# A two-layer hybrid block on one core: four-tile routing in fewer VectorE steps, the shared expert's products in quarters, and one direction's pairs of heads made ready one after the other

## The reference

```python
for l in range(DEPTH):
    last = l == DEPTH - 1
    hx = modulate(rmsnorm(x, g_mix[l]), ...)            # hc likewise from ctx
    y_x, y_c = hybrid_mixer(hx, hc, ..., not last)      # attention, mLSTM, RWKV7; merged, @ w_out
    x = x + mod_x[2] * y_x
    hx = modulate(rmsnorm(x, g_ffn[l]), ...)
    f = moe_ffn(hx and, but for the last layer, hc)
    x = x + mod_x[5] * f
return rmsnorm(x, g_final)

# the third branch, in each direction d = 0, 1:
w = -jax.nn.softplus(-(w0[d] + jnp.tanh(wl_d) @ w2[d])) - 0.5
decay, a = jnp.exp(-jnp.exp(w)), jax.nn.sigmoid(a0[d] + al_d @ a2[d])
kd = k * (1 + (a - 1) * k_a)
# and behind both: (norm(y) + bonus) * (sigmoid(gl) @ g2), the output gate

def moe_ffn(xf, ...):                                   # 64 experts, 8 groups
    scores = jax.nn.sigmoid(xf @ w_router)
    # the 4 best groups, then the 8 best experts in them
    _, eidx = lax.top_k(masked, TOP_K)
    wts = scores[eidx] / sum * ROUTED_SCALE
    return routed_experts(xf, eidx, wts, ...) + swiglu(xf, w_s_gate, w_s_up, w_s_down)
```

## Time and profile before

| | |
|---|---|
| median of 3 runs | 2645.62 us (2644.52 to 2645.91) |
| the profiled execution's own time | 2642.83 us |
| its span, first to last instruction | 2640.6 us |
| mean granted clock of TensorE | 0.953 |
| moved by DMA | 599.72 MB, mean 227 GB/s |
| chain that ended last | PE 82%, DMA 7%, DVE 5%, issue 3%, ACT 2% |

### The profile page before, as it was taken

The page is one execution under the profiler, slowest core; times in us unless marked ns, Lnnn a source line. Parts: engine busy times, 40 slices in busy tenths (PEclk is TensorE's granted clock), DMA queues, the critical chain, the costliest instruction groups (busy, mean ns, idle before and its releaser), DMA issues.

```text
span 2640.6 us, 41238 instructions
## 1 busy us (share of the span) xinstructions
PE 2402.9 (91%) x17286; PEld 1365.7 (52%) x17286; DVE 785.4 (30%) x1929; ACT 570.4 (22%) x1132; POOL 146.3 (6%) x154
## 2 busy tenths in 40 slices
PE   7999988999998898999998799988999799967997
PEld 3466477644445443333333556767788644433444
DVE  1364455311114431111111525555411521111112
ACT  3455223300002011111111144433210111100111
POOL 0000000000000111111111000000000011100100
PEclk9999999999997799999999899999999699988999
DMA  7101142411102699999999631122331599999993
GB/s 321 71 10 41 37 157 103 188 64 64 64 0 110 243 422 420 413 406 424 403 408 393 260 146 67 70 70 94 143 147 64 204 393 423 419 408 417 413 423 163
DMA packets 67640, 599.72 MB, mean 227 GB/s; under 512 B 13182, under 2 KB 13310, under 8 KB 25600
## 3 DMA queue, kind: packets, MB, share of 16 engines
q1 hardware_dynamic: 50032, 555.09, 51.9%
q0 software_dynamic: 17424, 41.99, 4.2%
HBM read 588.63 MB, written 26.75 MB: 233 GB/s over the span
## 4 chain that ended last, share of the span: by engine, by line
PE 82%; DMA 7%; DVE 5%; issue 3%; ACT 2%; another core or an unknown queue 0%; SPq 0%; ACTq 0%; DVEq 0%
PE bank L1870 10%; PE bank L1345 9%; PE bank L2296 7%; PE bank L292 6%; PE bank L1885 5%; PE bank L2310 3%; PE bank L1360 3%; PE bank L1350 3%; PE bank L2316 3%; PE bank L384 3%; DMA ring<-in_wexp 2%; DMA arena<-in_wexp 2%; PE bank L1034 2%; PE bank L1049 2%; PE bank L309 1%
## 5 line engine op out<-in xcount | busy, mean ns | idle before, releaser
L1870 PE MATMUL bank<-ring,arena 128*32 128x512 f32 (+2 forms) x1248 | 297.5, 610 | 16.5 <-issue 15.2
L1345 PE MATMUL bank<-normed,ring 128*128 128x512 f32 (+1 forms) x768 | 255.5, 486 | 0.0
L2296 PE MATMUL bank<-ring,arena 128*32 128x512 f32 (+2 forms) x832 | 193.4, 621 | 18.1 <-issue 16.6
L1345 PEld LDWEIGHTS bank<-normed,ring 128*128 128x128 f32 x768 | 145.9, 190 | 101.8 <-issue 91.8
L1870 PEld LDWEIGHTS bank<-ring,arena 128*32 128x32 f32 (+2 forms) x1248 | 94.7, 131 | 154.0 <-issue 152.0
L292 PE MATMUL bank<-normed,ring 128*128 128x512 f32 (+1 forms) x416 | 160.5, 544 | 0.0
L1870 PE MATMUL bank<-branches,arena 128*32 128x512 f32 (+2 forms) x400 | 134.3, 594 | 6.3 <-issue 6.3
L1885 PE MATMUL bank<-arena 128*32 128x512 f32 (+2 forms) x384 | 112.8, 596 | 7.0 <-DMA arena<-in_wexp 3.3
L292 PEld LDWEIGHTS bank<-normed,ring 128*128 128x128 f32 x416 | 78.4, 190 | 77.8 <-issue 75.3
L2060 DVE TENSOR_TENSOR arena<-bank,arena 128x256 f32<-128x256 f32 x43 | 18.3, 425 | 324.0 <-ACT arena L1979 324.0
L2296 PE MATMUL bank<-normed,arena 128*32 128x512 f32 (+1 forms) x256 | 92.9, 644 | 21.0 <-issue 18.1
(11 more groups left out here) (484 smaller groups left out, 3828.5 us busy)
## 6 DMA issues: line engine op xcount, KB each, us to landing
ring<-in_wexp SPq DMA_DIRECT2D x87, 2048.0 KB, 14.5
ring<-in_wst SPq DMA_DIRECT2D x54, 2048.0 KB, 8.4
arena<-in_wexp SPq DMA_DIRECT2D x70, 1024.0 KB, 20.4
branches<-in_wexp SPq DMA_DIRECT2D x31, 2048.0 KB, 13.8
ring<-in_wexp SPq DMA_DIRECT2D x60, 1024.0 KB, 12.1
normed<-in_wexp SPq DMA_DIRECT2D x12, 2048.0 KB
arena<-expert_rows SPq DMA_DIRECT2D x6, 2048.0 KB, 11.0
branches<-expert_rows SPq DMA_DIRECT2D x2, 2048.0 KB, 14.4
```

The lines of the kernel that those rows point to most:

```text
L1345: last = nc.tensor.matmul(ps[2 * (n % 4)][:, c0:], wg[:, k, i * P:(i + 1) * P], H[:, k, c0:], start=(k == 0), stop=(k == KD - 1))
L1870: last = nc.tensor.matmul(ps[2 + s][r0:r1, :], XT_[:, s, k * P + r0:k * P + r1], wt[:, k, :], start=(k == 0), stop=(k == KD - 1))
L2296: last = nc.tensor.matmul(ps[5][r0:r1, :], XT_[:, s, k * P + r0:k * P + r1], w[:, k, :], start=(k == 0), stop=(k == KD - 1))
```

## The change

1. **Third branch.** VectorE runs one loop over the pairs: pair 0 with scan, difference, and all its products, then pair 1. On ScalarE the sigmoid of the output gate moves from direction 0 to direction 1, and the copies of the values stand behind the exponentials of direction 0's pair 0.
2. **Routing on VectorE.** The running count of the marks (`r_cs`) goes. The places `r_at` are multiplied by the marks, and a MAX8 for each tile gives the eight places of a token in falling order. The one-hots of a tile are made in two wide operations, in two buffers of eight. The number of the choice is multiplied in by ScalarE, one activation for each one-hot, and TensorE waits for those (`ro["hc"]`). The positions are read from PSUM where they were copied.
3. **Routing on TensorE.** The counts come ahead of the positions, which fill in behind; `shared_gate_up` is cut in quarters (m, up): one ahead of the counts, two ahead of the one-hot products, one behind.
4. **Expert stages.** The shared expert's weights, and in the last layer those of the pinned experts, are asked for ahead of the stores of the flipped rows. The wait for the shared hidden part moves behind the first unit's gate and up product (in the last layer its first half stays ahead). In the last layer the shared down product moves behind unit 0's hidden flips; `down(0)` is asked for behind the fifth expert's parts.
5. **Last layer's start.** The first two chunks and the small weights don't wait for `sh["res"]`.
6. **Norms.** `norm_act_rs` starts with an Ln of a constant.

The diff, cut to its core, its indentation shortened; the buffers' places and the signals' counts are left out.

```diff
@@ -263,6 +263,7 @@
 def norm_act_rs(act, ch, l, w, c0):
+    ch.link(nc.scalar.activation(arena(4640, 1), cn("eps", 1), ACT.Ln))
@@ -1150,17 +1151,18 @@
-        if d == 0:
+        if d == 1:
...
-            for pr in PAIRS:
-                act.wait_ge(rw["tok"], l * RW["tok"] + pr + 1)
-                nc.scalar.activation(VT[pr][:, :, :], ps[4 + pr][:, :].rearrange("p (c f) -> p c f", c=NC), ACT.Copy).then_inc(rw["tokc"], 1)
...
+            if d == 0 and pr == 0:
+                for q in PAIRS:
+                    act.wait_ge(rw["tok"], l * RW["tok"] + q + 1)
+                    nc.scalar.activation(VT[q][:, :, :], ps[4 + q][:, :].rearrange("p (c f) -> p c f", c=NC), ACT.Copy).then_inc(rw["tokc"], 1)
@@ -1439,33 +1440,42 @@
+    shared_gate_up(pe, l, 0, 0)
...
-    for t in range(t0, TT):
-        for u in range(t0, t + 1):
-            nc.tensor.matmul(ps[2][:, t * E:(t + 1) * E], cn("before", P) if u == t else ones, r_sel[:, u, :],
-                             start=(u == t0), stop=(u == t))
...
+    def positions(t):
+        for u in range(t0, t + 1):
+            last = nc.tensor.matmul(ps[2][:, t * E:(t + 1) * E], cn("before", P) if u == t else ones, r_sel[:, u, :],
+                                    start=(u == t0), stop=(u == t))
+        return last
+    for t in range(t0, TT - 2):
+        positions(t)
...
+    positions(TT - 2)
...
-    shared_gate_up(pe, l, 0)
+    positions(TT - 1).then_inc(ro["pos"], 1)
+    shared_gate_up(pe, l, 0, 1)
+    shared_gate_up(pe, l, 1, 0)
...
-        pe.wait_ge(ro["hot"], l * RO["hot"] + i + 1)
-        nc.tensor.matmul(ps[0][:, 0:PLAN[l].n], r_hot[:, i % HOT, :], r_val[:, i % HOT, 0:PLAN[l].n],
+        b = (i // HOT) % 2
+        pe.wait_ge(ro["hc"], l * RO["hc"] + 2 * (TT - t0) + i + 1)
+        nc.tensor.matmul(ps[0][:, 0:PLAN[l].n], r_hot[:, b, k, :], r_val[:, b, k, 0:PLAN[l].n],
...
-    shared_gate_up(pe, l, 1)
+    shared_gate_up(pe, l, 1, 1)
@@ -1480,6 +1490,11 @@
+    for n, t in enumerate(range(t0, TT)):
+        act.wait_ge(ro["hot"], l * RO["hot"] + n + 1)
+        for k in range(HOT):
+            part = r_val[:, n % 2, k, 0:PLAN[l].n]
+            nc.scalar.activation(part, part, ACT.Copy, scale=cn("choice", 1, n * TOPK + k)).then_inc(ro["hc"], 1)
@@ -1505,8 +1520,9 @@
-    ch.add(V.tensor_tensor(q, pos, bcast(cap, 1, n_t), ALU.subtract))
...
+    dve.wait_ge(ro["pos"], l * RO["pos"] + 2)
+    ch.link(V.tensor_tensor(q, pos, bcast(cap, 1, n_t), ALU.subtract))
@@ -1566,10 +1582,6 @@
-    for t in range(t0, TT):
-        ch.add(V.tensor_tensor_scan(out=r_cs[:, t, :], data0=ones[:, 0:E], data1=r_sel[:, t, :], initial=0.0, op0=ALU.mult, op1=ALU.add))
-    ch.settle()
-    ch.add(V.tensor_tensor(r_cs[:, t0:, :], r_cs[:, t0:, :], r_sel[:, t0:, :], ALU.mult))
@@ -1586,24 +1598,21 @@
-    chosen = [(t, k) for t in range(t0, TT) for k in range(TOPK)]
-    for i, (t, k) in enumerate(chosen):
-        ch.add(V.scalar_tensor_tensor(r_junk[:, i % 2, :], r_cs[:, t, :], float(k + 1), r_at[:, t, :], ALU.is_equal, ALU.mult,
-                                      accum_out=r_dk[:, t, k:k + 1]))
-        ch.settle()
+    ch.link(V.tensor_tensor(r_keyed[:, t0:, :], r_at[:, t0:, :], r_sel[:, t0:, :], ALU.mult))
+    for t in range(t0, TT):
+        ch.add(V.max(r_dk[:, t, :], r_keyed[:, t, :]))
+    ch.settle()
...
-    for i, (t, k) in enumerate(chosen):
-        if i >= HOT:
-            dve.wait_ge(ro["hotm"], l * RO["hotm"] + i - HOT + 1)
-        ch.add(V.tensor_scalar(r_hot[:, i % HOT, :], cn("count", P), r_p[:, t, k:k + 1], None, ALU.is_equal))
-        ch.settle()
-        V.tensor_scalar(r_val[:, i % HOT, 0:at.n], cn("count", at.n), r_u[:, t, k:k + 1], cn("choice", 1, (t - t0) * TOPK + k),
-                        ALU.is_equal, ALU.mult).then_inc(ro["hot"], 1)
-    dve.wait_ge(ro["hotm"], l * RO["hotm"] + len(chosen))
+    for n, t in enumerate(range(t0, TT)):
+        if n >= 2:
+            dve.wait_ge(ro["hotm"], l * RO["hotm"] + (n - 1) * HOT)
+        ch.link(V.tensor_tensor(r_hot[:, n % 2, :, :], bcast(cn("count", P), 1, HOT), bcast(r_p[:, t, :], 2, P), ALU.is_equal))
+        V.tensor_tensor(r_val[:, n % 2, :, 0:at.n], bcast(cn("count", at.n), 1, HOT), bcast(r_u[:, t, :], 2, at.n), ALU.is_equal).then_inc(ro["hot"], 1)
+    dve.wait_ge(ro["hotm"], l * RO["hotm"] + n_t * HOT)
@@ -1708,21 +1717,23 @@
-def shared_gate_up(pe, l, m):
+def shared_gate_up(pe, l, m, up):
...
-    if m == 0:
+    if m == 0 and up == 0:
...
-    for up in range(2):
-        for k in range(KD):
-            last = nc.tensor.matmul(ps[4 + 2 * up + m][:, c0:], w[:, k, up * FE + m * P:up * FE + (m + 1) * P], H[:, k, c0:],
-                                    start=(k == 0), stop=(k == KD - 1))
-    last.then_inc(sh["gu"], 1)
+    for k in range(KD):
+        last = nc.tensor.matmul(ps[4 + 2 * up + m][:, c0:], w[:, k, up * FE + m * P:up * FE + (m + 1) * P], H[:, k, c0:],
+                                start=(k == 0), stop=(k == KD - 1))
+    if up:
+        last.then_inc(sh["gu"], 1)
...
+    sp.wait_ge(mg["o"], l * MG["o"] + KD)
+    sp.dma_start(GU_W[3], wexp[l, E, :, 0:GU_N]).then_inc(sh["w"], 16)
@@ -1733,8 +1744,6 @@
-    sp.wait_ge(mg["o"], l * MG["o"] + KD)
-    sp.dma_start(GU_W[3], wexp[l, E, :, 0:GU_N]).then_inc(sh["w"], 16)
@@ -1852,7 +1861,6 @@
-    pe.wait_ge(sh["hid"], l * SHN["hid"] + 4)
@@ -1919,6 +1927,8 @@
+        else:
+            pe.wait_ge(sh["hid"], l * SHN["hid"] + 4)
@@ -2048,11 +2058,14 @@
-    for m in range(2):
+    def shared_hidden(m):
         dve.wait_ge(sh["sig"], l * SHN["sig"] + m + 1)
...
+    shared_hidden(0)
@@ -2078,6 +2091,7 @@
+    shared_hidden(1)
@@ -2147,9 +2161,6 @@
-    for n in range(NX):
-        sp.wait_ge(ro["hc"], l * RO["hc"] + 2 * n + 2)
-        sp.dma_start(hx[l][n * P:(n + 1) * P, :], HTB[:, n, :]).then_inc(ro[f"hs{n}"], 16)
@@ -2164,18 +2175,21 @@
+    for n in range(NX):
+        sp.wait_ge(ro["hc"], l * RO["hc"] + 2 * n + 2)
+        sp.dma_start(hx[l][n * P:(n + 1) * P, :], HTB[:, n, :]).then_inc(ro[f"hs{n}"], 16)
...
+    fifth = sp.value_load(EJI[0:1, 4:5], min_val=0, max_val=E)
+    gate_up(fifth, 4, gu5_in[4][0])
...
+    sp.wait_ge(ro["dk"], l * RO["dk"] + 1)
+    down(fifth, 4, dn5_in[4][0])
...
-    fifth = sp.value_load(EJI[0:1, 4:5], min_val=0, max_val=E)
-    gate_up(fifth, 4, gu5_in[4][0])
-    sp.wait_ge(ro["dk"], l * RO["dk"] + 1)
-    down(fifth, 4, dn5_in[4][0])
@@ -2273,13 +2287,7 @@
-    pe.wait_ge(sh["hid"], l * SHN["hid"] + 4)
-    pe.wait_ge(*shared_down_in)
-    wt = DN5[0].rearrange("p (k m) -> p k m", k=2)
-    for m in range(KD):
-        for k in range(2):
-            last = nc.tensor.matmul(acc(m), wt[:, k, m * P:(m + 1) * P], SH[:, k * T + TC:(k + 1) * T], start=(m % 2 == 0 and k == 0), stop=False)
-    last.then_inc(sh["gu"], 1)
+    pe.wait_ge(sh["hid"], l * SHN["hid"] + 2)
@@ -2353,8 +2361,17 @@
+    def shared_down():
+        pe.wait_ge(*shared_down_in)
+        wt = DN5[0].rearrange("p (k m) -> p k m", k=2)
+        for m in range(KD):
+            for k in range(2):
+                last = nc.tensor.matmul(acc(m), wt[:, k, m * P:(m + 1) * P], SH[:, k * T + TC:(k + 1) * T], start=(m % 2 == 0 and k == 0), stop=False)
+        last.then_inc(sh["gu"], 1)
...
+    pe.wait_ge(sh["hid"], l * SHN["hid"] + 4)
@@ -2367,6 +2384,8 @@
+        elif u == 0:
+            shared_down()
@@ -2575,9 +2594,9 @@
-        if l:
-            sp.wait_ge(sh["res"], l * SHN["res"])
...
+            if l and n == 2:
+                sp.wait_ge(sh["res"], l * SHN["res"])
```

20 lines of the change are left out of this document (10 added, 10 removed).

## The result

| | before | after |
|---|---|---|
| median of the runs | 2645.76 us (4 runs, 2644.52 to 2652.57) | 2611.18 us (4 runs, 2607.23 to 2615.38) |
| profiled execution, its span | 2642.83, 2640.6 | 2611.15, 2609.0 |
| mean granted clock | 0.953 | 0.961 |

The ratio is 0.9864, interval 0.9842 to 0.9887: 36 us less by the ratio, 34.6 by the medians, where 24.1 were forecast. The sign was right, and the mechanisms were as forecast but for the clock over the one-hot products and the length of one DMA stop; the size was not. Timed again beside the experiments, the same kernel gave 2611.55 us (0.9865, 0.9844 to 0.9886). That leaves out one slow run of five, 3112.52 us at a granted clock of 0.743.

The account below looks back on a forecast made before the run. Routing stages were taken to count in full, the last layer's expert stage to be bound by its DMA weight stream. 14 + 5.3 + 4.8 + 0.3 - 0.3 = 24.1 us less, giving 2621.5 us against 2645.6; range 2611 to 2633.

Parts of the forecast that it names:

- The step that failed: First layer's routing: clock falls two microseconds into the one-hot products, 2 us per 16 rows at full clock, 3.9 at half.
- rival A: Routing: clock stays high since the quarter follows the flips; 8 us more in first layer, 4 in last, 2609; chance 0.13.
- the slow starts of the quarters: First layer's routing: shared products start at low clock, costing 1.9, 1.9 and 2.3 us.
- The wait for the shared hidden: First layer, before unit 0's first flips: TensorE no longer waits, 2.2 us gained.
- The stop before down(0): Last layer: SyncE waits there for the shared down product; DMA runs dry at 2120 and is back at 2125.
- Rival B: Last layer: the new stop eats its whole gain and the first layer gives 10 us; 2631, chance 0.17.
- the forecast's 3.4: Last layer: what the 5.3 us sum leaves out of the 8.7 us gained at the shared products' end.
- Third branch: Pair 0 made in full first: 1.5 and 1.15 us in the first layer, 0.9 and 1.3 in the last; sum 4.8.
- Rival C: Third branch: no gain, as pair 0 waits for exponentials that start no earlier; 4.8 us less, 2626; chance 0.06.
- rival D: Routing: 48 ScalarE scalings become a dependent chain costing 36 us, so the kernel is slower, 2658; chance 0.03.
- final norm: Final norm: the extra Ln loads the table early but costs 0.3 us, where Ln follows the load at once.
- the last layer's early chunks: Last layer's start: two chunks come during the combine, but modulated rows pace the first projection; 0.3 us gained.

Follow-up runs that it names:

- order_only: The kernel before with only the change's TensorE order in the routing, its early loads, and positions read where TensorE leaves them; 2638.33 us, ratio 0.9961.
- change_again: The changed kernel with nothing changed, timed again beside the experiments; 2611.55 us.
- late_chunks: The changed kernel with the wait for the first layer's sum back ahead of the last layer's first chunk; 2611.00 us, ratio 0.9874.
- route_all: The kernel before with the change's whole routing and early loads, shared down product still ahead of the last layer's unit 0; 2621.45 us, ratio 0.9891.
- the two timed kernels: The kernel before with the change's part 1 alone, 2641.85 us; and the changed kernel without part 1, 2615.78 us.
- down_first: The changed kernel with the last layer's shared down product ahead of unit 0 again; 2609.57 us, ratio 0.9862.
- gap: The changed kernel with one quarter of the shared products instead of two ahead of the one-hot products, two behind; 2625.09 us, ratio 0.9928.
- third_undone: The changed kernel without part 1, the third branch as before; 2615.78 us, ratio 0.9884.

## Why the prediction missed, step by step

- **The step that failed** is "with the clock falling two microseconds into these products, as it does now". I carried the clock of the earlier trace rows over to products that no longer come at the pace of VectorE's pairs. It stayed at 1.00 in both traced executions of the change: the last tile was done 4 us early in the first layer (871.5 against 867.56), and in the last layer the shared products were done 4 us early. The case stood as rival A, for 8 and 4 us, but with the wrong reason (the early quarter behind the flips, which order_only rules out) and a chance of 0.13. That its 2609 lies so near the measured time is partly luck: the two routings together brought 9.6 us more than forecast, not its 12, and not from its terms.
- Rival A's own sizes in the first layer: the slow starts of the quarters did stay, 8.60, 15.54 and 8.83 us against 6.9, 13.8 and 6.9 at full clock, 5.4 in all, where 6.1 had been taken; so 0.7 of its 8 us came from there and not 6, and the late tiles brought 4 and not 2, since ScalarE and VectorE wait for their products in turn.
- The wait for the shared hidden gave 2.8 us and not 2.2: the shared products now end 1.3 us ahead of unit 0 (879.40 to 880.68), before it was 4.1.
- **Last layer.** The stop before down(0) was right in place and cause, and too long by 2.5 us. Counted from the fourth gate/up load's issue (2077.67), DMA was to run dry after 15.9 us and did after some 17; the shared down product was to end after 19.5 us and ended after 17.9, since the prediction kept most of TensorE's waits there (1.39 and 0.68 us) and they are gone. Rival B, that the stop would eat the whole gain, is out: 9.4 of 12.7 us came through. Of the 3.3 lost, 1.6 lie ahead of the last gate/up product and 1.7 behind it, where the last unit's down product took 5.35 us instead of 3.65, its first 3.6 us at a clock of 0.61. That is not the change's doing: change_again and late_chunks show 3.65 there too, and order_only and route_all, whose weight stream has no such stop, show 5.35. So it is luck that the 3.3 lost are as large as the forecast's 3.4.
- In the prediction's working for this stream 1.35 MB by 2118 should be 1.55 (259 GB/s over 6 us of the earlier trace rows); its 2132.9 goes with 1.55.
- **Third branch.** 1.5 us in the first layer's direction 0 as worked out; in the last layer TensorE's waits shrank from 5.16 to 3.77 us and from 6.73 to 5.44, 1.4 and 1.3, where 0.9 and 1.3 were forecast. In all 6.1 and 4.2 us in the two timed kernels, around 4.8. The table's -3.9 us in the last layer is no cost of the change but the stop described below: the stretch that holds it is 6.1 us longer than before, and -3.9 + 6.1 is the forecast's 2.2. Rival C is out.
- **Slower** (rival D): the scalings took 0.26 us each and formed no dependent chain.
- The rest: final norm as forecast; the last layer's early chunks 1.0 us instead of 0.3. The 1.2 us up to the first norm's sum come from the first input's arrival (TensorE's first wait is 9.75 us instead of 10.24) and from TensorE's first 32 rows behind it (5.70 us instead of 6.37), which the change doesn't touch.

The whole: in the two profiled executions the change brought 7.5 us more than forecast, 9.6 of them in the two routings and 2.1 less in all other stretches together. By the medians it is 10.5; the profiled execution before was 2.9 us below its median and the one after at its median, which is the difference. Of the 2.1 less, the stop alone took some 6 the other way.

## What to carry to other kernels

When a change replaces many short, spaced products by tight groups, don't take TensorE's clock for them from the stage before the change: look at what the engine does just ahead of them and how far apart they come, and give the high clock a chance of its own that is as large. Work for TensorE that can be cut in pieces is best put where it fills its waits, since such a wait was paid twice here, by itself (2.7 us) and by the slow start behind it (1.5 us). A wait in an in-order DMA queue costs only the time by which the loads issued ahead of it run out first; count both ends of it from the same issue, and look for waits that the change itself takes away. And before two profiled executions are compared row by row, look for stops that only one of them has.

## What was not expected of the hardware

TensorE sometimes stops for 1 to 3.5 us in a dense part of the third branch, with nothing in its program to wait for, at the same instruction each time. Of the changed kernel, TensorE's order of time and windows:

```profile
1848.94 0.98 PE L1035 MATMUL bank<-arena 64*64 64x64 f32 x27
1853.40 0.34 PE L1035 MATMUL bank<-arena 64*64 64x64 f32 x5 [3.49 <-issue]
```

```profile
1846.00:1850.00 4.00, 3.91 (x136) 3.83 (x131) 2.03 (x4) 0.00 (x0) 0.00 (x0) 1.00 0.95 317
1850.00:1853.00 3.00, 0.00 (x0) 0.00 (x0) 0.54 (x1) 0.00 (x0) 0.00 (x0) 1.00 0.66 273
1853.00:1856.00 3.00, 2.60 (x41) 2.48 (x40) 1.26 (x2) 1.16 (x2) 0.00 (x0) 0.61 0.04 16
```

and of late_chunks at the same place, which ran through:

```profile
1844.98 1.15 PE L1035 MATMUL bank<-arena 64*64 64x64 f32 x32
```

```profile
1839.00:1842.00 3.00, 3.00 (x45) 1.47 (x47) 0.19 (x1) 0.69 (x2) 0.00 (x0) 1.00 0.10 38
1842.00:1848.00 6.00, 5.99 (x180) 5.82 (x177) 3.85 (x6) 1.20 (x2) 0.00 (x0) 1.00 0.94 343
```

The stop lies inside a 2 MB weight transfer and ends about when DMA falls quiet; behind it the clock is low for a while. In the last layer there is one at this instruction in five of the fourteen traces (2.39 to 3.49 us), in the first layer at another in all but one (1.23 to 2.26 us; 0.68 in the last of them). That TensorE's instructions come late behind the weights would fit, but late_chunks had the same transfer begin as long ahead of the same instruction (4 us) and did not stop, so the transfer alone doesn't decide, and nothing was run to test it. The cost can be read from all traces: from TensorE's wait at the start of this stage (1.52 us at L1034 or L1035) to its 1.74 us wait behind the branch (L1112 or L1113) the last layer's direction 1 takes 60.3 to 61.3 us in the nine traces without the stop and 66.8 to 67.9 in the five with it, some 6 us. That may be much of why single runs of one kernel lie so far apart: four of the profiled executions without it (down_first, gap, late_chunks, third_undone) are the fastest of their kernel, none of the five with it is.
